# First feed-forward layer in seven half-size products for eight, from the third group on

## The reference, cut to what matters

```python
D_FF = 4 * D_MODEL                       # 4096
...
    x = x + rms_norm(mix, g_post_mix)
    h = rms_norm(x, g_pre_ffn)
    f = jnp.square(jax.nn.relu(h @ w_ff1)) @ w_ff2
    return x + rms_norm(f, g_post_ffn)
```

## Time and profile before

| | us |
|---|---|
| median of 3 runs | 1717.76 (1717.62 to 1719.08) |
| the profiled execution, its time | 1716.92 |
| its span, first to last instruction | 1715.0 |
| busy in the span: PE | 1698.2 (99%) |
| DVE | 1104.3 (64%) |
| ACT | 783.1 (46%) |
| POOL | 585.6 (34%) |

### The profile page before, as it was taken

How to read it: one execution, slowest core, us unless ns; L and a number is a source line. 1 busy time by engine, 2 the same in 40 slices (tenths; PEclk the granted TensorE clock), 3 DMA queues, 4 the chain that set the end, 5 groups by cost and what they waited for, 6 DMA issues and landing times.

```text
span 1715.0 us, 27666 instructions
## 1 busy us (share of the span) xinstructions
PE 1698.2 (99%) x9346; PEld 1459.2 (85%) x9346; DVE 1104.3 (64%) x1973; ACT 783.1 (46%) x1323; POOL 585.6 (34%) x289
## 2 busy tenths in 40 slices
PE   9999999999999999999999999999999999999998
PEld 7877778888888788889999998888888879999997
DVE  5655565333333587688787695566675588688684
ACT  5666543222222433653443354565655453353354
POOL 3232325444445378241210203442523440220221
PEclk9999999999999999999999999999999999999999
DMA  7542213222222242233322333231212233342331
GB/s 197 119 99 85 74 59 126 94 93 96 98 98 87 74 129 87 74 111 99 112 94 90 110 99 111 74 99 49 86 61 74 75 100 96 101 132 74 98 111 50
DMA packets 153712, 162.61 MB, mean 95 GB/s; under 512 B 10627, under 2 KB 114679, under 8 KB 153631
## 3 DMA queue, kind: packets, MB, share of 16 engines
q1 hardware_dynamic: 149167, 158.66, 30.1%
q10 hardware_dynamic: 4464, 2.89, 0.5%
HBM read 157.84 MB, written 3.67 MB: 94 GB/s over the span
## 4 chain that ended last, share of the span: by engine, by line
PE 92%; DVE 4%; ACT 2%; issue 1%; DMA 0%; SPq 0%; DVEq 0%; ACTq 0%
PE ps L1675 49%; PE ps L2080 21%; PE ps L2105 10%; PE ps L1696 2%; PE ps L2187 1%; PE ps L2023 1%; PE ps L1704 1%; PE ps L1894 1%; PE ps L1913 1%; DVE ps L2715 1%; PE ps L1800 0%; PE ps L1806 0%; PE ps L2220 0%; PE ps L1877 0%; DMA lnmult<-const_lnmult 0%
## 5 line engine op out<-in xcount | busy, mean ns | idle before, releaser
L835 POOL TENSOR_TENSOR wlo<-raw,whi 128x1024 fp32r<-128x1024 f32 x92 | 224.8, 2451 | 339.3 <-ACT whi L952 324.0
L1675 PE MATMUL ps<-h_hi,wlo 128*128 128x512 f32 x800 | 323.0, 404 | 6.5 <-DVE gate L2814 5.7
L1675 PE MATMUL ps<-h_hi,whi 128*128 128x512 f32 x800 | 313.1, 391 | 0.0
L1675 PE MATMUL ps<-h_lo,whi 128*128 128x512 f32 x800 | 312.9, 391 | 0.0
L952 ACT ACTIVATE whi<-raw 128x1024 fp32r<-128x1024 f32 x170 | 176.5, 1055 | 251.1 <-PE ps L1675 241.7
L842 POOL TENSOR_TENSOR wlo<-raw,whi 128x1024 fp32r<-128x1024 f32 x60 | 146.9, 2464 | 293.3 <-ACT whi L952 170.2
L1675 PE MATMUL ps<-m_hi,wlo 128*128 128x512 f32 x544 | 214.9, 395 | 0.0
L1675 PE MATMUL ps<-m_hi,whi 128*128 128x512 f32 x544 | 211.9, 390 | 0.0
L1675 PE MATMUL ps<-m_lo,whi 128*128 128x512 f32 x544 | 211.8, 389 | 0.0
L1675 PEld LDWEIGHTS ps<-h_hi,wlo 128*128 128x128 f32 x800 | 150.7, 188 | 38.5 <-issue 8.1
L1675 PEld LDWEIGHTS ps<-h_hi,whi 128*128 128x128 f32 x800 | 150.6, 188 | 33.0
(11 more groups left out here) (411 smaller groups left out, 3938.9 us busy)
## 6 DMA issues: line engine op xcount, KB each, us to landing
raw<-in_ffn_w SPq DMA_DIRECT2D x264, 256.0 KB, 2.9
raw<-in_w_ff SPq DMA_DIRECT2D x128, 256.0 KB, 2.7
raw<-in_hg_w_in SPq DMA_DIRECT2D x64, 256.0 KB, 3.0
raw<-in_w_in SPq DMA_DIRECT2D x40, 256.0 KB, 5.2
raw<-in_cp_w_in SPq DMA_DIRECT2D x24, 256.0 KB, 2.8
raw<-in_w_out SPq DMA_DIRECT2D x16, 256.0 KB, 3.0
raw<-in_cp_w_out SPq DMA_DIRECT2D x16, 256.0 KB, 3.0
raw<-in_hg_w_out SPq DMA_DIRECT2D x16, 256.0 KB, 2.9
```

Source lines behind the costliest of these rows:

```text
L835: pool.tensor_tensor(wlo[:, u % RING, :, :], raw[:, u % RING, :, :], whi[:, u % RING, :, :].bitcast(F32), ALU.subtract).then_inc(unit_lo, 1)
L1675: mm = pe.matmul(ps[:, b, :], wt[:, s, a, m * P:(m + 1) * P], xt[:, kts[a], :], start=starts and a == 0 and i == 0, stop=last)
```

## The change

**What is computed.** Groups 0 and 1 stay as they are. The up products of groups 2 to 7 are made in 12 blocks of 256 columns (`F_BLOCKS`; block j is numbered 0 to 11, two a group). A block's weights are quarters a11, a21, a12, a22 of 512 rows by 128 columns; with the tokens in quarters too (features 0 to 511 or 512 to 1023, tokens 0 to 255 or 256 to 511), seven products of a 512x128 quarter by 512x256 tokens take the place of eight. Tags: y1, u2, u3, p5, c11, c12, c21, in this order.

**Tokens.** Of the seven token operands three are parts of `h` as it is and four are sums of parts, made once: ACT makes `f1` (4 copies with the gain), DVE makes `f3`, `f1`, `f2`, `f1` again in 13 operations (`ffn_token_sums`), ACT their hi parts, DVE their lo parts (`ffn_token_lo`, four of 128x1024). They stand in DVE's queue between the hidden features of group 1 and the drains of down 0.

**A turn.** A loop of 5 turns (`F_TURNS`) runs two blocks and one down: PE does block 2i+1, block 2i+2, then the down of group i+2. Block 0 stands ahead of the loop, block 11 behind it. A block uses the banks 0 to 3 for seven products: odd blocks 0, 1, 2, 3, 0, 1, 2, even blocks 3, 0, 1, 2, 3, 0, 1. A product can begin when the one that had its bank before is drained.

**DVE per block:** 4 sums of quarters (`ffn_sum`), 7 lo parts (`ffn_low`), and 9 operations that put the products together (`ffn_u2` to `ffn_c21`; ACT drains y1); per tile of hidden features a square and a rest (`ffn_hidden`). The four `hid` tiles are gone: `hid` is `sq` in the first two groups, and `ss` and `sq` hold the square and the second pair of `relu`.

**Slots.** The forms' hi and lo parts stand in 11 slots of 128x512 (`F_SLOTS`): 8 in `whi`, `wlo` and 3 in `fwhi_more`, `fwlo_more`, which lie over `f1`. The down weights of a turn use 8 of these slots, ACT and POOL split them one slot at a time (8 POOL operations of 128x512 a turn, where there were 4 of 128x1024 for it).

**POOL's end of the layer.** The four parts of `second_table` now stand behind a wait for the last hidden feature (`hid_lo` at 32) and among the last four units.

The diff, cut to its core:

```diff
+F_SLOTS = 11
+F_BLOCKS = 2 * (FFN_GROUPS - 2)
+F_TURNS = FFN_GROUPS - 3
...
+def ffn_banks(j):
+    at = (0, 1, 2, 3, 0, 1, 2) if j % 2 else (3, 0, 1, 2, 3, 0, 1)
+    return [((tag, j), b) for tag, b in zip(TAGS, at)]
...
@@ gpsimd
-            lo_parts(0, U_CPIN - 8)
+            lo_parts(0, U_FFN + 16)
...
+            with pool.Fori(0, F_TURNS) as i:
+                for d in range(8):
+                    s = ffn_form_slot(2 * FORMS + FORMS + d)
+                    u = U_FFN + 22 + d // 2
+                    pool.wait_ge(form_hi, at(i, F_TURN, F_DOWN + d + 1))
+                    pool.tensor_tensor(ffn_lo_slot(s), raw[:, u % RING, d % 2, :], ffn_hi_slot(s).bitcast(F32), ALU.subtract)\
+                        .then_inc(down_lo, 1)
+            pool.sem_inc(unit_lo, F_LATER - 16)
             pool.wait_ge(consts_in, 16 * 3)
-            for j in range(8):
-                lo_part(U_CPIN - 8 + j)
-                if j % 2 == 0:
-                    table(1, j // 2)
+            for j in range(4):
+                lo_part(U_FFN + F_LATER + j)
+                if j == 0:
+                    pool.wait_ge(filled[ffn_bank(F_LAST, "c21")], ffn_nth(F_LAST, None, "c21"))
+                    pool.wait_ge(hid_lo, 4 * FFN_GROUPS)
+                table(1, j)
@@ scalar
+            with act.Fori(0, F_TURNS) as i:
+                ffn_high(2, 0, i)
+                ffn_hidden_high(0, 0, i)
+                ffn_high(2, 1, i)
+                ffn_y1(1, i)
+                for f in range(2, FORMS):
+                    ffn_high(2, f, i)
+                ffn_down_high(0, i)
+                ffn_hidden_high(0, 1, i)
+                ffn_down_high(1, i)
+                ffn_hidden_high(1, 0, i)
+                ffn_y1(2, i)
+                ffn_hidden_high(1, 1, i)
+                for d in range(2, 8):
+                    ffn_down_high(d, i)
+                for f in range(FORMS):
+                    ffn_high(3, f, i)
@@ tensor
+            ffn_up(4, 0)
+            ffn_down(8, 0, 0)
+            ffn_down(12, 1, 1)
...
+                    pe.wait_ge(form_lo, at(i, 2 * FORMS, FORMS * j + f + 1))
...
+                    pe.wait_ge(drained[b], ffn_nth(j, i, TAGS[f]) - 1)
...
+            ffn_products(0, 0)
+            with pe.Fori(0, F_TURNS) as i:
+                ffn_products(1, 2, i)
+                ffn_products(2, 1, i)
+                ffn_turn_down(i)
+            ffn_products(F_LAST, 2)
+            pe.sem_inc(unit_begun, F_LATER - 16 - 1)
+            ffn_down(F_LATER, FFN_GROUPS - 1, 0)
@@ vector
+            def ffn_forms(y, i, after):
+                ffn_sum(y, 1, i)
+                ffn_sum(y, 2, i)
+                ffn_low(y, 0, i)
+                ffn_sum(y, 3, i)
+                ffn_low(y, 1, i)
+                after(1)
+                ffn_low(y, 2, i)
+                ffn_sum(y, 4, i)
+                after(2)
+                ffn_low(y, 3, i)
+                after(3)
+                ffn_low(y, 4, i)
+                after(4)
+                ffn_low(y, 5, i)
+                after(5)
+                ffn_low(y, 6, i)
...
+            with dve.Fori(0, F_TURNS) as i:
+                ffn_hidden(0, 0, i)
+                ffn_during(1, 2, i)
+                ffn_c21(1, i)
+                ffn_hidden(0, 1, i)
+                ffn_hidden(1, 0, i)
+                ffn_u2(2, i)
+                ffn_hidden(1, 1, i)
+                ffn_u3(2, i)
+                ffn_p5(2, i)
+                ffn_c11(2, i)
+                ffn_c12(2, i)
+                ffn_c21(2, i)
+                ffn_forms(3, i, lambda n: ffn_down(i + 2, halves=(0,)) if n == 4 else None)
+                ffn_down(i + 2, halves=(1,))
```

More of the change, by code:

```diff
@@ new lines, in ffn_turn_down @@
+            def ffn_turn_down(i):
+                for q in range(4):
+                    h, p = q // 2, q % 2
+                    s = [ffn_form_slot(F_DOWN + 2 * q + a) for a in range(2)]
+                    pe.wait_ge(down_lo, at(i, 8, 2 * q + 2))
+                    begun = False
+                    for a, m in [(a, m) for m in range(4) for a in range(2)] if p else [(a, m) for a in range(2) for m in range(4)]:
+                        kt = 2 * p + a
+                        if m == 0:
+                            pe.wait_ge(hid_lo, at(i, 4, 8 + kt + 1))
+                        if p == 0 and a == 0:
+                            pe.wait_ge(drained[4 + m], before("ffndown", ("d", h, m), i + 2))
+                        for r, (wt, xt) in enumerate(((ffn_lo_slot(s[a]), m_hi), (ffn_hi_slot(s[a]), m_lo), (ffn_hi_slot(s[a]), m_hi))):
+                            last = p == 1 and a == 1 and r == 2
+                            mm = pe.matmul(ps[:, 4 + m, :], wt[:, m * P:(m + 1) * P], xt[:, kt, :],
+                                           start=kt == 0 and r == 0, stop=last)
+                            if not begun:
+                                mm.then_inc(form_used, 2 if q else 1)
+                                begun = True
+                            if last:
+                                mm.then_inc(filled[4 + m], 1)
@@ L2627, in ffn_up, with ffn_down @@
                     parts(m)
-            def ffn_down(g, first=False, last=False):
-                for h in range(2):
+            def ffn_down(g, first=False, last=False, halves=(0, 1)):
+                for h in halves:
                     for m in range(4):
@@ new lines, in ffn_p5, with ffn_c11 @@
+            def ffn_p5(j, i=None):
+                ffn_filled(j, "p5", i)
+                ffn_drained(j, "u3", i)
+                dve.tensor_tensor(ffn_kept(j)[:, 1, HALF:], ffn_part(j, "p5"), fu3[:, :], ALU.add)
+                dve.tensor_tensor(fu2[:, :], ffn_part(j, "p5"), fu2[:, :], ALU.add)\
+                    .then_inc(drained[ffn_bank(j, "p5")], 1)
+            def ffn_c11(j, i=None):
+                ffn_filled(j, "c11", i)
+                dve.scalar_tensor_tensor(out=ffn_kept(j)[:, 0, 0:HALF], in0=ffn_part(j, "c11"), scalar=0.0,
+                                         in1=rs[:, 0:HALF], op0=ALU.max, op1=ALU.mult)\
+                    .then_inc(drained[ffn_bank(j, "c11")], 1)
@@ new lines, in ffn_c12 @@
+            def ffn_c12(j, i=None):
+                ffn_filled(j, "c12", i)
+                ffn_drained(j, "p5", i)
+                out = ffn_kept(j)[:, 0, HALF:]
+                dve.tensor_tensor(out, ffn_part(j, "c12"), fu2[:, :], ALU.add)\
+                    .then_inc(drained[ffn_bank(j, "c12")], 1)
+                ffn_drained(j, "c12", i)
+                dve.scalar_tensor_tensor(out=out, in0=out, scalar=0.0, in1=rs[:, HALF:], op0=ALU.max, op1=ALU.mult)\
+                    .then_inc(relu_ready, 1)
```

386 lines of the change are left out of this document (330 added, 56 removed).

## The result

| | before | after |
|---|---|---|
| median, us | 1718.24 (4 runs, 1717.62 to 1719.08) | 1751.31 (4 runs, 1750.03 to 1752.75) |
| profiled span, us | 1715.0 | 1748.9 |
| mean granted clock of TensorE in it | 0.998 | 0.987 |
| busy, us: PE | 1698.2 | 1705.5 |
| DVE | 1104.3 | 1252.7 |

The changed kernel takes 1.0194 times as long, 95% interval [1.0181, 1.0207]: 33.1 us slower, where 23.5 was forecast. The time lies 1.3 us above the upper end of the range. Two rows of the table already say that something is missing in the forecast: PE has 9.7 us less to do at the old pace and is nevertheless busy 7.3 us longer, and its clock is lower.

A forecast was written before the change was run, and what follows sets the result against it. The prediction took PE's matmuls to bound the kernel. Its terms, -9.7 + 21.9 + 8.2 + 3.1 = +23.5 us on the profiled 1716.92, with the median 0.84 above that, gave 1741 us; range 1721 to 1750.

The forecast's parts named there:

- PE's -9.7: Changed layer: 130.7 us of 512-column matmuls leave and 120.9 us of 256-column ones come, -9.7 us.
- The turn: Loop: DVE, held up by POOL, drains u2 and u3 late; 4.3 us a turn, 4.8 in the first, +21.9 us.
- The gap ahead of c12: Even block of each turn: u2 is done at 19.6, its bank wanted at 17.3; PE waits 2.3 us.
- The gap ahead of c21: Even block of each turn: u3 is done at 23.0, its bank wanted at 21.0; PE waits 2.0 us.
- The start: Down 0: DVE's token sums, held up by POOL, delay copies from banks 4 to 7; with down 1, +8.2 us.
- The 0.4 at down 1: PE waits 0.4 us since DVE is still behind with four lo parts of 128x1024.
- The end: Down 7: POOL's table delays the second unit's lo part, 2.8 us; +3.1 us in all.
- the 0.3: Down 7: 0.3 us where DVE's sums of squares meet POOL's table parts.
- the sum itself: Whole change: -9.7 + 21.9 + 8.2 + 3.1 = +23.5 us.
- the seven products do not run at 0.1200: Rival: the new 256-column matmuls take other than 0.1200 us each; given nothing, as two layers already run so.
- worse: Rival: POOL's six later operations catch DVE operations that matter, or forms come late; 6 to 7 us a turn, 1750 to 1756; chance 0.08.
- The chances: Whole kernel against the one before: slower 0.84, same 0.07, faster 0.09.

The follow-up runs named there:

- the best order: Changed kernel with u2/u3 drained before the pairs, first-half copies earlier, token sums split, and down 7's lo parts and copies moved earlier: 1709.35 us, ratio 0.9952.

## Why the prediction was off in size and right in the rest

- **PE's -9.7.** Right. At full clock a block of 84 takes 10.07 us, forecast 10.08 from the earlier trace rows, and a turn 42.05, forecast 41.9; and the best order ends 8.5 us under the kernel before.
- **The turn.** The mechanism and its moments were right. In turn 2 block 3 begins at 389.8 (the down product of turn 1 ends there); u2 ends at 409.14, that is at 19.3 where 19.6 was forecast, and u3 at 412.5, 22.7 for 23.0. POOL's six later operations begin at 15.5, forecast from 15 on. The gap ahead of c12 is 2.16 in every turn, forecast 2.3. The gap ahead of c21 is 0.9 to 1.9, forecast 2.0: where c12 itself ran slowly, its 12 matmuls took up to 1.2 us longer and used up so much of the wait (in turn 4 it ran at full clock, and the gap is 1.93). Gaps and slow c12 together are 10.8 + 6.3 + 3.8 = 20.9 us, forecast 21.9. That c12's slowness hid behind the second wait is luck: the forecast had no slow c12. Two slips of reckoning change nothing: the operations with two SBUF inputs are 30 a turn (8 + 14 + 4 + 4), not 32, and four turns of 4.3 and one of 4.8 are 22.0.
- **The start.** 7.7 for 7.8; three operations of DVE were held by POOL, as said. The 0.4 at down 1 did not show.
- **The end.** 2.8 for 2.8; the 0.3 did not show.
- **The step that failed** is the sum itself: it prices each matmul that runs behind a wait at the distances of the earlier trace rows, 0.2269 and 0.1200 us, which come from stretches in which PE never stood still. The rival *the seven products do not run at 0.1200* was given nothing, on the same grounds. Behind the waits they ran at 0.213. The grounds didn't cover the case: the kernel before has one wait of 4.05 us, and behind it its matmuls too ran at half the clock, but in rows that the prediction doesn't read. That cost 9.5 us that no term held: 1.65 in down 0, 7.8 in c21 and the down products of the turns, and 0.1 in down 7 (the slow c12, 3.8, lay inside what was forecast as waiting). It is nearly the whole miss: 23.5 + 9.5 = 33.0, for 33.1 measured; beyond it 1.6 us of small gaps stand against terms that were 1.8 us too large.
- **The rival *worse*** had a span of times, 1750 to 1756, that holds the result, but not its mechanism: it had 6 to 7 us of waiting a turn, and there are 3.4. The right time would have been right for a wrong reason.
- **The chances** on the side were right: slower, since the waits of the turns alone outweigh the -9.7.
